# Sliding-window attention of layer 1: two heads at a time, with projection tiles between the pairs

## The reference, cut to what matters

```python
def swa_mixer(h, wq, wk, wv, q_norm_w, k_norm_w, sinks, wo):
    q = rms_norm((h @ wq).reshape(b, l, kv, grp, d), q_norm_w) * (d ** -0.5)
    k = rms_norm((h @ wk).reshape(b, l, kv, d), k_norm_w)
    v = (h @ wv).reshape(b, l, kv, d)
    ...
    pm = sink_softmax(jnp.where(mmask, sm, -jnp.inf), sink[None, :, :, None, None])
    om = jnp.einsum('bkgij,bjkd->bikgd', pm.astype(v.dtype), vm).reshape(b, N_META, SWA_HEADS * d)
    ...
    p = sink_softmax(jnp.concatenate([s_meta, s_band], -1), sink[None, None, :, :, None, None])
    orr = (jnp.einsum('bnkgim,bmkd->bnikgd', p[..., :N_META], vm)
           + jnp.einsum('bnkgij,bnjkd->bnikgd', p[..., N_META:], vband))
    return jnp.concatenate([om, orr], 1) @ wo
```

## Time and profile before

| | us |
|---|---|
| median of 3 runs | 1401.7 |
| lowest and highest run | 1398.02, 1426.21 |
| the profiled execution, its own time | 1396.14 |
| its span | 1394.3 |
| TensorE busy in the span | 1322.1 (95%) |
| VectorE, ScalarE, GpSimd busy | 901.7, 666.4, 173.6 |

### The profile page before, as it was taken

One profiled execution on the slowest core, in us unless ns is written; L12 is line 12 of the kernel. 1 busy time (PEld: TensorE's weight loads), 2 busy tenths in 40 slices (PEclk: granted clock), 3 DMA queues, 4 the chain that ended last, 5 costly groups with the idle time before them and its releaser, 6 DMA issues.

```text
span 1394.3 us, 27491 instructions
## 1 busy us (share of the span) xinstructions
PE 1322.1 (95%) x10279; PEld 1248.8 (90%) x10279; DVE 901.7 (65%) x1672; ACT 666.4 (48%) x1162; POOL 173.6 (12%) x219
## 2 busy tenths in 40 slices
PE   6988989999999989999999998999999878999996
PEld 6968978999999856999999987999999766999996
DVE  6956347877755555788854665667555687776553
ACT  5544224555534246655544454565444366555431
POOL 4112313000012100200012000300011123200011
PEclk9979989999999969999999999999999999999998
DMA  6423704555654400555665542465566520566662
GB/s 231 157 85 70 128 18 149 180 168 178 203 176 139 134 1 29 172 189 184 204 199 169 177 128 91 142 193 187 186 184 187 190 77 27 173 189 185 183 187 69
DMA packets 60354, 206.31 MB, mean 148 GB/s; under 512 B 6000, under 2 KB 14320, under 8 KB 60144
## 3 DMA queue, kind: packets, MB, share of 16 engines
q1 hardware_dynamic: 56000, 200.81, 47.0%
q10 hardware_dynamic: 4272, 4.35, 1.0%
HBM read 200.95 MB, written 4.19 MB: 147 GB/s over the span
## 4 chain that ended last, share of the span: by engine, by line
PE 84%; DVE 9%; ACT 4%; issue 2%; DMA 0%; DVEq 0%; POOLq 0%; POOL 0%; ACTq 0%
PE bank L300 24%; PE bank L302 23%; PE bank L301 23%; PE bank L1259 3%; DVE w_lo L265 3%; PE bank L1274 2%; ACT w_hi L256 2%; PE bank L1234 2%; DVE cb L628 1%; PE bank L1071 1%; PE bank L1087 1%; PE bank L1025 1%; PE bank L1085 1%; DVE x_lo L376 1%; DVE h L422 0%
## 5 line engine op out<-in xcount | busy, mean ns | idle before, releaser
L265 DVE TENSOR_TENSOR w_lo<-raw,w_hi 128x1024 fp32r<-128x1024 f32 (+1 forms) x358 | 458.8, 1282 | 241.9 <-ACT w_hi L256 241.6
L256 ACT ACTIVATE w_hi<-raw 128x1024 fp32r<-128x1024 f32 (+1 forms) x358 | 388.1, 1085 | 326.5 <-PE bank L302 303.7
L300 PE MATMUL bank<-x_hi,w_hi 128*128 128x256 f32 (+2 forms) x1784 | 518.0, 290 | 16.8 <-DVE x_lo L376 12.2
L302 PE MATMUL bank<-x_hi,w_lo 128*128 128x256 f32 (+2 forms) x1784 | 510.4, 286 | 0.0
L301 PE MATMUL bank<-x_lo,w_hi 128*128 128x256 f32 (+2 forms) x1784 | 510.1, 286 | 0.0
L300 PEld LDWEIGHTS bank<-x_hi,w_hi 128*128 128x128 f32 x1784 | 339.9, 191 | 26.9 <-DVE w_lo L265 12.0
L302 PEld LDWEIGHTS bank<-x_hi,w_lo 128*128 128x128 f32 x1784 | 340.3, 191 | 0.0
L301 PEld LDWEIGHTS bank<-x_lo,w_hi 128*128 128x128 f32 x1784 | 339.5, 190 | 0.3
L300 PE MATMUL bank<-m_hi,w_hi 128*128 128x256 f32 x512 | 143.4, 280 | 0.0
L301 PE MATMUL bank<-m_lo,w_hi 128*128 128x256 f32 x512 | 142.9, 279 | 0.0
L302 PE MATMUL bank<-m_hi,w_lo 128*128 128x256 f32 x512 | 142.9, 279 | 0.0
(11 more groups left out here) (275 smaller groups left out, 1789.8 us busy)
## 6 DMA issues: line engine op xcount, KB each, us to landing
raw<-w_up SPq DMA_DIRECT2D x88, 512.0 KB, 3.5
raw<-w_mlp_up SPq DMA_DIRECT2D x64, 512.0 KB, 3.6
raw<-w_mlp_down SPq DMA_DIRECT2D x64, 512.0 KB, 4.0
raw<-w_down SPq DMA_DIRECT2D x32, 704.0 KB, 4.1
raw<-w_mix_in SPq DMA_DIRECT2D x29, 512.0 KB, 3.6
raw<-w_moba_in SPq DMA_DIRECT2D x24, 512.0 KB, 3.6
raw<-w_swa_in SPq DMA_DIRECT2D x12, 512.0 KB, 3.6
raw<-w_mix_out SPq DMA_DIRECT2D x8, 512.0 KB, 4.1
```

Source lines behind the costliest of these rows:

```text
L256: nc.scalar.activation(w_hi[:, slot, 0:WIDTHS[g]], raw[:, slot, 0:WIDTHS[g]], ACT.Copy).then_inc(hi_ready, 1)
L265: nc.vector.tensor_tensor(w_lo[:, slot, 0:WIDTHS[g]], raw[:, slot, 0:WIDTHS[g]], w_hi[:, slot, 0:WIDTHS[g]].bitcast(F32), ALU.subtract).th ...
L300: nc.tensor.matmul(out, whi, xh, start=(chunk == 0), stop=False)
L302: mm = nc.tensor.matmul(out, wlo, xh, start=False, stop=end)
```

## The change

Layer 1 gets helpers of its own. What it does:

- The columns of `swa_in` are reordered (keys, the first query tile, values, the other queries), its tiles go round two banks (0 and 1), and only tiles 0 to 5 run ahead of the attention. Tiles 6 to 11 are set into steps 0 to 5 of a loop of nine steps, one for each pair of heads and one to finish. Pair p's queries come from tile 4 + p (pair 0's from tile 2).
- Queries are no longer multiplied by their norms. `query_sums` gets the sums of squares per token by three narrow matmuls, ScalarE takes the mean (`squares_mean`), GpSimd raises it to the power -0.5 (`rsqrt`), and VectorE's score step uses it as a scale. The norm weights of queries and keys are folded into the keys. Keys are normalised once by one fp32 matmul per tile in place of two fp32r ones for each of ten tiles.
- The sink is an extra column of the scores, so its exp and its sum come with those of the scores. The probabilities of the meta keys of both heads go to a small block `smx`, which is transposed and multiplied once per pair (`extra_turn`, `extra_values`). Value matmuls alternate between the two heads of a pair, whose outputs lie on partitions 0 to 63 and 64 to 127 of one bank. One output bank serves all pairs.
- The meta queries' softmax moves to steps 6 and 7.
- Chunks 0 to 5 of the first two tiles of `swa_out` are issued in step 8; `pe_linear` adds chunks 6 and 7.
- GpSimd clears five blocks after tile 0 is read out, and computes each power ahead of the next square.

```diff
+            if lin is LIN["swa_in"]:
+                return bank[(lin.tile0 + t) % 2]
...
+            part = part or (0, lin.chunks)
+            if part[0] == 0 and lin.tile0 + t >= BANKS:
+                behind = 2 if lin is LIN["swa_in"] else BANKS
+                pe.wait_ge(evac_done, lin.tile0 + t - behind + 1 + i * step)
...
-            for t in range(min(4, tiles)):
+            begun = 2 if name == "swa_out" else 0
+            for t in range(begun):
+                pe_tile(pe, lin, t, ready=ready if t == 0 else None, part=(SWA_EARLY, KD))
+            for t in range(begun, min(4, tiles)):
...
+        def pair_scores(pe, at, p):
+            if p:
+                at.wait(pe, "max", 4 * p)
+            for g, c0, w in ((1, 0, at.wa), (0, at.wa, at.wb)):
+                for j in range(2):
+                    r = slice(HD * j, HD * j + HD)
+                    mm = nc.tensor.matmul(SCORE_BANKS[j][:, c0:c0 + w], at.q(p, r, g), at.k(p, r, g),
+                                          start=True, stop=True)
+                    if g == 0:
+                        mm.then_inc(at.s["scores"], 1)
+        def pair_turn(pe, at, p):
+            for j in range(2):
+                u = 2 * p + j
+                at.wait(pe, "p", 2 * u + 2)
+                if p:
+                    at.wait(pe, "pt", 2 * p - 1 + j)
+                for dst, c in ((0, at.c0 + at.first), (P, at.first), (2 * P, at.first + P)):
+                    tr = nc.tensor.transpose(TURN_BANKS[j][:, dst:dst + P], at.slot(u)[:, c:c + P], ident)
+                tr.then_inc(at.s["turned"], 1)
+        def pair_values(pe, at, p, extra=None):
+            at.wait(pe, "pt", 2 * p + 2)
+            if p:
+                pe.wait_ge(y_lo_ready, Y0[at.y] + p)
+            for chunk, src, q0, w in ((0, 0, 0, 2 * P), (1, 2 * P, P, P)):
+                for j in range(2):
+                    r = slice(HD * j, HD * j + HD)
+                    mm = nc.tensor.matmul(OUT_BANK[r, q0:q0 + w], at.v(p, j, chunk),
+                                          at.pt[:, p % 2, j, src:src + w], start=(chunk == 0),
+                                          stop=(chunk == 1 and extra is None), skip_group_check=True)
+            if extra is not None:
+                mm = extra(p)
+            mm.then_inc(at.s["o"], 1)
...
+        def pair_reduce(dve, at, p):
+            for j in range(2):
+                u = 2 * p + j
+                if p >= 2:
+                    at.wait(dve, "turned", 2 * (p - 1))
+                if at.extra:
+                    nc.vector.tensor_copy(at.slot(u)[:, at.wa:at.c0 + at.wb + 1:at.wb + 1],
+                                          prm_col("sinks", u).to_broadcast([P, 2]))
+                at.wait(dve, "scores", u + 1)
+                for (x, c0, w), src, bias in zip(at.parts(), (0, at.wa), (at.bias_a(u), at.bias_b(u))):
+                    nc.vector.tensor_tensor_reduce(
+                        out=at.slot(u)[:, c0:c0 + w], in0=SCORE_BANKS[j][:, src:src + w], in1=bias,
+                        scale=at.scale(u, x), scalar=GONE, op0=ALU.add, op1=ALU.max,
+                        accum_out=at.st[:, u, x:x + 1]).then_inc(at.s["max"], 1)
+                at.wait(dve, "max", 2 * u + 2)
+                sink = prm_col("sinks", u) if at.extra else GONE
+                nc.vector.tensor_scalar(at.st[:, u, 2:4], at.st[:, u, 0:2], sink, -1.0, ALU.max,
+                                        ALU.mult).then_inc(at.s["negmax"], 1)
+        def pair_norm(dve, at, p):
+            for j in range(2):
+                u = 2 * p + j
+                at.wait(dve, "exp", 2 * u + 2)
+                nc.vector.reciprocal(at.st[:, u, 6:8], at.st[:, u, 4:6]).then_inc(at.s["rec"], 1)
+                at.wait(dve, "rec", u + 1)
+                if at.first:
+                    nc.vector.tensor_tensor(
+                        smx[:, p % 2, :, HD * j:HD * j + META],
+                        at.slot(u)[:, 0:2 * at.c0].rearrange("p (x c) -> p x c", x=2)[:, :, 0:META],
+                        at.st[:, u, 6:8].unsqueeze(2).to_broadcast([P, 2, META]), ALU.mult)
+                for x, c0, w in at.parts():
+                    c0, w = c0 + at.first, w - at.first
+                    nc.vector.tensor_scalar(at.slot(u)[:, c0:c0 + w], at.slot(u)[:, c0:c0 + w],
+                                            at.st[:, u, 6 + x:7 + x], None,
+                                            ALU.mult).then_inc(at.s["p"], 1)
...
+            def square(f, t, slot):
+                pool.wait_ge(evac_done, SWA0 + t + 1)
+                nc.gpsimd.tensor_tensor(slot, qs[:, f, :], qs[:, f, :], ALU.mult).then_inc(S("swa_sq"), 1)
+            def rsqrt(t):
+                pool.wait_ge(S("ms_ready"), t + 1)
+                nc.gpsimd.tensor_tensor(rqv[:, 4 * t:4 * t + 4], msv[:, 4 * t:4 * t + 4], halves[:, 0:4],
+                                        ALU.pow).then_inc(S("rq_ready"), 1)
+            square(8, 0, sqr[:, 0, :])
+            square(9, 1, sqr[:, 1, :])
+            square(0, 2, swa_square(0))
+            rsqrt(0)
+            pool.wait_ge(S("swa_pe"), 1)
+            for t in range(1, 8):
+                if t >= 3:
+                    pool.wait_ge(S("rq_sum"), t - 2)
+                if t > 1:
+                    rsqrt(t - 1)
+                square(t, 4 + t, swa_square(t))
+            rsqrt(7)
...
+                pe.wait_ge(S("swa_sq"), t + 3)
+                if t:
+                    pe.wait_ge(S("ms_ready"), t)
+                if t > 1:
+                    pe.wait_ge(S("firsts_copied"), t - 1)
+                sel = C("head64")[:, 19:21]
+                for x, g in ((0, 1), (1, 0)):
+                    nc.tensor.matmul(bank[7][:, 4 * t + 2 * x:4 * t + 2 * x + 2],
+                                     swa_square(t)[:, META + P * g:META + P * (g + 1)], sel,
+                                     start=True, stop=True)
+                nc.tensor.matmul(bank[7][0:META, 64 + 2 * t:66 + 2 * t], swa_square(t)[:, 0:META], sel,
+                                 start=True, stop=True).then_inc(S("rq_sum"), 1)
+            def extra_turn(p):
+                pe.wait_ge(S("ms_ready"), p + 2 if p < 6 else 9)
+                if p:
+                    pe.wait_ge(S("firsts_copied"), p)
+                for dst, x in ((0, 1), (P, 0)):
+                    tr = nc.tensor.transpose(bank[7][:, 2 * P + dst:2 * P + dst + P], smx[:, p % 2, x, :], ident)
+                tr.then_inc(S("firsts_turned"), 1)
+            def extra_values(p):
+                pe.wait_ge(S("firsts_copied"), p + 1)
+                return nc.tensor.matmul(OUT_BANK[:, 0:2 * P], vmbd[:, p // 4, :], ptx[:, p % 2, :], start=False,
+                                        stop=True, skip_group_check=True)
...
+            for p in range(SWA_STEPS):
+                if p < HEADS // 2:
+                    pe.wait_ge(evac_done, SWA0 + (3 if p == 0 else 5 + p))
+                    pair_scores(pe, swa, p)
+                if p:
+                    pair_turn(pe, swa, p - 1)
+                    extra_turn(p - 1)
+                if p == 8:
+                    pe.wait_ge(S("meta_dve"), 5)
+                    pe_tile(pe, out, 0, ready=early, part=(0, SWA_EARLY))
+                if p < 6:
+                    pe_tile(pe, lin, 6 + p)
+                if p + 1 < HEADS // 2:
+                    query_sums(p + 1)
+                if p == 6:
+                    pe.wait_ge(S("swa_dve"), 6)
+                    pe.wait_ge(evac_done, SWA0 + 12)
+                    for t in range(HEADS // 2):
+                        mm = nc.tensor.matmul(META_IN[0:META, 32 * t:32 * (t + 1)], qs[:, t, 0:META],
+                                              kbd[:, t // 4, :], start=True, stop=True)
+                    mm.then_inc(S("meta_pe"), 1)
+                if p == 7:
+                    pe.wait_ge(S("meta_dve"), 3)
+                    for t in range(HEADS // 2):
+                        tr = nc.tensor.transpose(META_OUT[:, META * t:META * (t + 1)],
+                                                 smm[:, t, :, :].rearrange("p j c -> p (j c)"),
+                                                 ident[0:META, 0:META])
+                    tr.then_inc(S("meta_pe"), 1)
+                if p:
+                    pair_values(pe, swa, p - 1, extra_values)
+                if p == 7:
+                    pe.wait_ge(S("meta_dve"), 4)
+                    for f in range(2):
+                        mm = nc.tensor.matmul(META_OUT[:, P + 4 * META * f:P + 4 * META * (f + 1)], vmbd[:, f, :],
+                                              ptm[:, 4 * META * f:4 * META * (f + 1)], start=True, stop=True)
+                    mm.then_inc(S("meta_pe"), 1)
+            pe.wait_ge(swa.s["max"], swa.before["max"] + 2 * HEADS)
+            pe_tile(pe, out, 1, part=(0, SWA_EARLY))
```

350 lines of the change are left out of this document (238 added, 112 removed).

## The result

The changed kernel takes 1378.97 us, the median of four executions (1376.26 to 1382.77). The ratio to the kernel before is 0.9844, with a 95% interval of 0.9823 to 0.9865, so it is 19 to 25 us faster. Executions of the kernel before at 1426 us and more are left out of that ratio.

The account below looks back on a forecast made before the run. The prediction took TensorE to bound the attention's second half, the first being the same work at half clock. Out-projection matmuls done at 530.5 instead of 552.9 gave a gain of 22.4 us, forecast 1377.5 us, range 1366 to 1391.

Parts of the forecast that it names:

- same: Outcome for the whole kernel: a time the measurement cannot tell from no change, within about 2% or 28 us; chance 0.77.
- faster: Outcome for the whole kernel: a gain past about 28 us, reached only by the cheaper-than-summed rival, gain 28 to 32; chance 0.2.
- A step with a tile: Attention loop, layer 1: TensorE's scores, transposes, tile, query sums and values sum to 7.3 us, covering VectorE and ScalarE.
- The start: Layer 1 up to step 0: TensorE waits 1.5 us for the keys' reciprocal; pair 0's transposes end at 470.0.
- rival 6: Wait at 457 to 460: the clock falls early, tiles 5 and 6 at half speed, 3 us less; no chance of its own.
- The tail: Last steps without tiles: waits show, VectorE's chain runs to 520.7, out-projection matmuls to 526.5 at full clock, 530.5 with slow clock.
- The fall of the clock behind the softmax's wait: Tail: TensorE under half busy from 511 to 519, so its clock falls near 515, adding 4 us.
- The end mark: Out-projection: the gain counted at its 36th matmul, 530.5 against 552.9 in the kernel before, 22.4 us.
- Values that do not overlap (2): Value matmuls: 0.85 us more in seven steps, gain 16, 1384 us; chance 0.17 together with the mode-change rival.
- Mode changes (3): TensorE's tiling changes in each step: 0.6 us a step, gain 18, 1382 us; chance 0.17 together with the non-overlapping values.
- A wait in every step (4): Attention steps: VectorE's output-bank read or ScalarE's loop makes 8.5 to 9 us, gain 10 to 14, 1388 us; chance 0.15.
- The dear power (5): GpSimd: from about 6 us a power sets the step; at 10 the kernel loses 7 us, 1407; chance 0.03.

Follow-up runs that it names:

- e5: Changed kernel with the first 14 columns of the meta queries' 16-column power taken a step earlier: 1380.48 us, ratio 0.9864 to the kernel before.
- e8: Changed kernel with eleven constant matmuls of 256 columns in TensorE's wait for the meta softmax: 1377.99 us, ratio 0.9855 to the kernel before.
- e4: Changed kernel without the early part of the out-projection, all its matmuls after the last pair: 1376.07 us, ratio 0.984 to the kernel before.
- e13: Changed kernel with both heads' value matmuls on the first 64 columns of the array: 1384.71 us, ratio 0.9843 to the kernel before.
- e2: Changed kernel with projection tiles 6 to 11 run before the first pair: 1383.79 us, ratio 0.9899 to the kernel before.
- e10: Changed kernel with four more 4-column powers on GpSimd ahead of the power of pairs 1 to 6: 1395.14 us, ratio 0.995 to the kernel before.

## Why the prediction was right and wrong

**The step that failed is the last one, from the forecast to the chances:** "A measurement of this kernel can tell about 2%, 28 us, from no change; the forecast lies inside." The forecast, 1377.5 and a gain of 22.4, was met by 1378.97 and a ratio that makes 21.8. The chances behind it gave 0.77 to "same" and 0.2 to "faster", and the kernel is faster, by far more than the measurement leaves open. Four executions give an interval of 0.2% on either side, 3 us, so a gain of 22 us is seven times what is uncertain. 28 us is the spread of the three times shown (1398 to 1426), not what a comparison can tell; two of the three agree within 0.3%. With a forecast gain of 22 and a range of 9 to 34, "same" deserved next to nothing.

**Sums that held.** A step with a tile: 7.3 forecast, 6.86 measured. By parts: scores 0.91 as said, tile 3.10 for 3.1, query sums 0.57 for 0.7, values 1.43 for 1.4, transposes 0.85 for 1.2: the drain that the earlier trace rows hold at the end of five transposes I had counted into each. The last step with a tile ends 65.1 us behind the start of the projection, as forecast (504.4 less 439.33), because five steps gave back what the start had lost (the first scores came 26.2 us behind the start of the projection and not 24.2). That the two agree is luck.

**The start.** TensorE's wait for the reciprocal was forecast at 1.5 and is 1.02. The clock fell there, rival 6; it costs 1.5 us, not 3, and not every time (first scores at 22.55 or 21.04), so it is a case inside the forecast rather than a rival.

**The tail.** The priced chain had one operation missing, the power of 16 columns. I had bounded the one of 4 columns (taken at 1, measured 1.01) and never asked what GpSimd does last: 2.89 us, for 2.24 of which VectorE waits; e5 took 2.7 off the path. The fall of the clock behind the softmax's wait came as forecast, between 516 and 517; I gave it 4 us, e8 measured 2.6. From the end of the last step with a tile to the 36th matmul of the out-projection it is 26.3 us where 26.1 were forecast: the missing power and the cheaper fall partly cancel, and that is luck too.

**The end mark was the wrong one.** "18 matmuls of the out-projection at 0.12 take 2.2, values 1.4, 18 more 2.2", compared with "the same 36 matmuls" of before. That counts matmuls done, as if TensorE set the out-projection's pace. It is paced by ScalarE and VectorE at 3.18 us a tile from the last result on; the earlier trace rows hold both terms, 1085 and 1282 ns, and I did not add them up with the residual's. Counted in that way the gain came out as summed, 22 us (552.9 less 439.33, against 531.6 less 440.24 after). By the right mark it is 20.4 (106.16 to 85.76), and the early part costs 3.0 us instead of gaining. The time, known to 3 us, can't tell the two marks apart; e4 did.

**The rivals.** Values that do not overlap (2): no; e13 shows the price it would have had, 0.64 a step. The reason I gave, that they alternate, is wrong: head by head they took the same 0.81. The Trainium skill ("TensorE: Matmul & The Clock Gate", Part 3) has three column tiles at 2.38 times the speed; two stand here at 1.8 times. The prediction's "by that the values would come to 1.4" does not follow from this figure: 2.38 over three tiles is 0.79 a tile, and 768 columns at that, with the 256 behind them, make an estimate of 1.6 us. Mode changes (3): the step's parts leave no 0.6 us for them; scores take 0.91 as in the earlier trace rows, and the tile 3.10 where six in a row take 3.03 each (e2). The Trainium skill ("TensorEngine Tiling (Array Packing)", Key Properties) has a drain at such a change; no row here shows more than the 0.1 to 0.2 at the first matmul of a kind, which the sums above contain. A wait in every step (4): none on TensorE. The dear power (5): a power was said to have 3.5 us free, and e10 makes it 3.0, its own 1.01 and 2.0 more. So it would have decided from 3 us a power on and not from 6; at 1.01 it never came near.

## What to carry to other kernels

Choose the mark at which a stage ends by asking what the next stage is paced by; here, work that TensorE did ahead of a chain on two other engines was worth nothing, and what it delayed cost its full length. When work of two kinds is interleaved, price the steps at both ends by themselves, down to each small operation in a row, since here the slack lay in the full steps. Before giving "same" a chance, compare the forecast gain with how closely repeated executions agree and not with the spread of those listed.

## What the hardware showed that I had not expected

- GpSimd's power goes by columns, not by elements, about 0.16 us each: 128 x 4 in 1.01 us, 16 x 2 in 0.69, 16 x 14 in 2.58, 16 x 16 in 2.89.
- fp32 matmuls on the two column halves of the array overlap whether issued by turns or head by head: 768 columns in 0.81 us, and 1.45 on one half.
- The same wait of 1.02 us on TensorE (1.01 in two) was followed by 3.4 us at a granted clock near 0.5 in six of ten executions and by none in four.
- In the kernel before, matmuls put into the waits of the norms did not keep the clock (0.76 over 480.00 to 492.80, TensorE busy 11.19 of 12.80 us), while eleven matmuls in one block, 4.92 us, kept it in the tail.
